# Fetching an expert's two rows with one gather of 8 KB per token, in a two-block transformer kernel

## The chip, the cores and the metric

The kernel runs as one program on one core of a Trainium2 chip. The metric is the time of one execution on the device, in microseconds (us). Three executions of the kernel before took 2143.99, 2161.14 and 2180.10 us; their median, 2161.14 us, is the time before. A profile of one execution shows what each engine did: TensorE (PE, matmuls), VectorE (DVE), ScalarE (ACT), GpSimd (POOL), SyncE (SP), and the 16 DMA engines that move data between HBM and SBUF.

## The reference, cut to what matters

A sequence of 256 tokens of width 1024 goes through a first block (modulated attention and pooling, then a convolutional feed-forward) and through a second model of two layers. Layer 0 has a hybrid attention (a sparse and a block-sparse one), layer 1 a latent attention with compressed keys. Each layer ends in a feed-forward of 16384 small experts, of which each token takes 16 in each of 8 heads. For a token `h` and its pick with table row `i` and weight `g` that is:

```
u = u_tab[i]                      # 1024 numbers, one row of 4 KB
v = v_tab[i]                      # 1024 numbers, one row of 4 KB
y += g * gelu(sum(u * h)) * v     # 8 heads x 16 picks for each token, in both layers
```

The rows are different for each token, so they are gathered by index. 2 layers x 256 tokens x 128 picks x 8 KB is 537 MB, three quarters of all that the kernel reads.

## The kernel before, in words

The program is written by hand engine by engine, with semaphores between engines. A function `order()` writes one list of steps, and each of the five engines walks the same list and does its own part of each step, in that order. An engine never takes a later step first: if its part of a step waits, all its later parts wait behind it.

**Tiles and picks.** Tokens form two tiles of 128, one token on each SBUF partition. A "round" is (layer, tile, head), and a pick is a round and a number j from 0 to 15, so there are 32 rounds and 512 picks. One gather (`L1699`, POOL) fetches for all 128 tokens the row of one table that their pick j names: 128 rows of 4 KB, 512 KB in all. There are 1024 gathers, 512 from each table. They land in a ring, `gring`, of NG = 16 slots of 4 KB on each partition. A gather waits until the slot's user 16 gathers earlier is done.

**A pick's work.** Step `u`: DVE multiplies the U row by the token and sums it (`dot`, L1537), which leaves one number on each partition in `acts`, and the slot is free. After 16 dots, step `gate`: ACT takes Gelu of the 16 numbers at once (L1054), DVE multiplies them by the 16 gate weights (L1544). Step `v`: for most picks ACT writes a 128x128 diagonal matrix of the 16 numbers' column (`diagonal`, L1063, one of four buffers, made two picks ahead), and PE multiplies it with the V row in two matmuls of 512 columns into an accumulating PSUM bank (L825 and L826). For the picks that `by_vector` names (odd j in the heads 0 to 3 except in the first two heads of all, and odd j in all heads of the last tile) DVE adds the scaled V row instead (L1556). The steps `v` of a round stand between the steps `u` of the next round, so V runs 16 picks behind U.

**What lies around.** The first block and the first tile's hybrid attention run before the first gather, until 556 us. After that the expert picks are dealt out between the steps of the rest (`together`, with `PACE`): while the experts of one tile run, the other tile's attention, its projections and its choice of experts (`pick`, on DVE, with one Exp on ACT, L1049) are computed. There are three such stages: layer 0 experts of tile 0 beside the hybrid attention of tile 1; layer 0 experts of tile 1 beside the latent attention of tile 0; layer 1 experts of tile 0 beside the latent attention of tile 1. At the end the experts of layer 1, tile 1 run with nothing beside them.

An attention is a series of 16 units, and the steps of unit u, the transposes of unit u-1 and the product with the values of unit u-2 stand together. A unit is: PE scores (L670), DVE adds the mask and takes the row maximum (L1338, L1345), ACT Exp (L1020), PE transposes (L566), ACT or DVE copy, PE product with the values (L687), DVE scaling (L1357). A projection (`mm`, L621) reads weights in loads of 1 MB, each with 4 x 128 rows of 512 numbers (2 KB), that SP issues into NW = 6 slots of `wring`. During the first block other parts of `gring` hold modulation vectors, gains and the last weights of the first feed-forward (`HELD`); their places are fixed column ranges.

## Time and profile before

| quantity | value |
|---|---|
| time of three executions, us | 2143.99, 2161.14, 2180.10 |
| median, us | 2161.14 |
| profiled execution: span from its first to its last instruction, us | 2111.6 |
| PE, DVE, ACT, POOL busy, us | 1648.0, 1375.4, 388.8, 1128.4 |
| gathers: packets, MB, share of the 16 DMA engines' time | 147456, 536.94, 65.0% |
| other loads: packets, MB, share | 106942, 182.85, 24.2% |
| first gather waits until, us | 556 |

The page has no other time of the profiled execution than its span, which is 49.5 us below the median of the three timed ones. The profile cuts the span in 40 slices of 52.8 us and says for each how busy an engine was. A gather has 128 data packets of 4 KB, eight on each DMA engine, and 16 small ones that raise the semaphore.

### The profile page before, as it was taken

The page shows a single profiled execution, that of the slowest core. Times are in us where ns is not written, and L with a number is a line of the kernel's source. Part 1 is how long each engine was busy: PE and PEld are TensorE (multiplying, and loading weights), DVE is VectorE, ACT ScalarE, POOL GpSimd, SP SyncE. Part 2 cuts the span into 40 slices and gives each one's busy share as a digit, 9 for nine tenths or more (in the row PEclk, how much of TensorE's full clock was granted, in tenths as well). Part 3 has the DMA queues.
Part 4 walks back from the last instruction along what each step waited for, and adds up shares of the span by engine and source line. Part 5 has one row for each costly group of instructions (what it writes and reads, how often), then busy time and mean ns, then how long its engine had stood idle before and what let it go on. Part 6 is the DMA issues. An engine that isn't in the chain of part 4 may idle for free.

```text
span 2111.6 us, 15758 instructions
## 1 busy us (share of the span) xinstructions
PE 1648.0 (78%) x4610; PEld 828.8 (39%) x4610; DVE 1375.4 (65%) x3269; ACT 388.8 (18%) x902; POOL 1128.4 (53%) x1028
## 2 busy tenths in 40 slices
PE   3997999998567978987876888878768996555565
PEld 1465887444233434432343433333434442111111
DVE  6564432142796695687757668776784887777775
ACT  1022000012121222222122222221322221100001
POOL 0000000000377577577766767776687777777773
PEclk9977999998789979999796999999788999887667
DMA  9851569162799999999999999999999999999997
GB/s 357 303 197 60 165 194 329 57 238 80 245 372 385 401 399 407 401 406 380 400 396 406 404 403 406 408 397 401 397 354 384 407 394 365 408 409 409 409 410 313
DMA packets 254483, 720.79 MB, mean 341 GB/s; under 512 B 24518, under 2 KB 49598, under 8 KB 253886
## 3 DMA queue, kind: packets, MB, share of 16 engines
q0 software_dynamic: 147456, 536.94, 65.0%
q1 hardware_dynamic: 106942, 182.85, 24.2%
q8 instruction: 38, 0.62, 0.1%
q14 instruction: 47, 0.39, 0.0%
HBM read 718.66 MB, written 1.05 MB: 341 GB/s over the span
## 4 chain that ended last, share of the span: by engine, by line
PE 40%; DMA 21%; POOL 17%; DVE 13%; issue 7%; ACT 2%; SPq 0%; POOLq 0%; DVEq 0%; ACTq 0%
POOL gring L1699 17%; DMA gring<-in_peer_v_dram,sel_idx 17%; PE PS L621 13%; PE PS L753 7%; PE PS L825 5%; PE PS L826 5%; DVE gring L1537 4%; PE PS L727 4%; PE PS L566 3%; DMA gring<-in_peer_u_dram,sel_idx 2%; DMA wring<-in_hyb_w_in_dram 1%; DVE xs L1556 1%; PE PS L670 1%; PE PS L687 1%; PE PS L706 1%
## 5 line engine op out<-in xcount | busy, mean ns | idle before, releaser
L1699 POOL DMA_INDIRECT gring<-in_peer_u_dram,sel_idx x512 | 566.0, 1105 | 725.1 <-DVE sel_g L1523 556.2
L825 PE MATMUL PS<-gring,diags 128*128 128x512 f32 x736 | 449.0, 695 | 321.3 <-DMA gring<-in_peer_v_dram,sel_idx 211.5
L1699 POOL DMA_INDIRECT gring<-in_peer_v_dram,sel_idx x512 | 562.2, 1098 | 230.3 <-issue 130.5
L1537 DVE CUSTOM_DVE_ANT_0 gring<-gring,hs 128x1024 f32<-128x1024 f32 x400 | 482.1, 1221 | 134.3 <-DMA gring<-in_peer_u_dram,sel_idx 133.1
L826 PE MATMUL PS<-gring,diags 128*128 128x512 f32 x736 | 434.2, 676 | 0.0
L621 PE MATMUL PS<-wring,hTs 128*128 128x512 f32 (+3 forms) x968 | 410.4, 574 | 9.8 <-DVE hTs L1125 4.3
L825 PEld LDWEIGHTS PS<-gring,diags 128*128 128x128 f32 x736 | 135.4, 210 | 545.4 <-issue 383.4
L621 PEld LDWEIGHTS PS<-wring,hTs 128*128 128x128 f32 x968 | 179.8, 195 | 219.8 <-issue 217.4
L826 PEld LDWEIGHTS PS<-gring,diags 128*128 128x128 f32 x736 | 158.8, 216 | 210.5 <-issue 210.5
L1063 ACT ACTIVATE diags<-consts,acts 128x128 f32<-128x128 f32 x368 | 136.4, 397 | 511.3 <-PE PS L826 476.8
L1537 DVE CUSTOM_DVE_ANT_0 gring<-gring,PS 128x1024 f32<-128x1024 f32 x112 | 136.4, 1220 | 70.4 <-DMA gring<-in_peer_u_dram,sel_idx 70.4
L753 PE MATMUL PS<-hTs,wring 128*128 128x256 f32 (+1 forms) x768 | 154.8, 365 | 1.9 <-DVE hTs L1101 1.9
L753 PEld LDWEIGHTS PS<-hTs,wring 128*128 128x128 f32 x768 | 137.5, 193 | 19.8 <-issue 2.3
L1556 DVE SCALAR_TENSOR_TENSOR xs<-gring,acts,xs 128x1024 f32<-128x1024 f32 x80 | 102.6, 1282 | 8.3 <-DMA gring<-in_peer_v_dram,sel_idx 8.1
L566 PE MATMUL PS<-consts,work 128*128 128x128 f32 (+1 forms) x344 | 67.2, 321 | 50.0 <-ACT work L1020 18.6
L950 ACT ACTIVATE work<-PS 128x512 f32<-128x512 f32 (+4 forms) x122 | 55.7, 463 | 222.0 <-PE PS L621 114.0
L1556 DVE SCALAR_TENSOR_TENSOR PS<-gring,acts,PS 128x1024 f32<-128x1024 f32 x62 | 79.9, 1288 | 12.3 <-DMA gring<-in_peer_v_dram,sel_idx 8.8
L566 PEld LDWEIGHTS PS<-consts,work 128*128 128x128 f32 (+1 forms) x344 | 48.5, 161 | 84.5 <-ACT work L1020 23.6
L1020 ACT ACTIVATE work<-work,small 128x128 f32<-128x128 f32 (+3 forms) x72 | 35.3, 490 | 226.2 <-DVE small L1345 226.2
L1148 DVE SCALAR_TENSOR_TENSOR gring<-wring,small,gring 128x512 f32<-128x512 f32 x84 | 63.1, 751 | 3.9 <-DMA wring<-in_w_ada_dram 1.1
L727 PE MATMUL PS<-gring,keep 128*128 128x512 f32 x120 | 55.0, 600 | 0.9 <-issue 0.9
L1338 DVE CUSTOM_DVE_ANT_0 work<-PS,consts 128x128 f32<-128x128 f32 (+1 forms) x72 | 25.5, 354 | 38.1 <-PE PS L670 37.4
(194 smaller groups left out, 1188.9 us busy)
## 6 DMA issues: line engine op xcount, KB each, us to landing
wring<-in_peer_w_q_dram SPq DMA_DIRECT2D x32, 1024.0 KB, 14.7
wring<-in_w_ada_dram SPq DMA_DIRECT2D x24, 1024.0 KB, 9.7
wring<-in_w_up_dram SPq DMA_DIRECT2D x44, 512.0 KB, 5.1
wring<-in_hyb_w_in_dram SPq DMA_DIRECT2D x20, 1024.0 KB, 8.3
wring<-in_w_in_dram SPq DMA_DIRECT2D x10, 1024.0 KB, 8.1
wring<-in_hyb_w_out_dram SPq DMA_DIRECT2D x8, 1024.0 KB, 19.2
gring<-in_peer_u_dram,sel_idx POOLq DMA_INDIRECT x512, 12.9
gring<-in_peer_v_dram,sel_idx POOLq DMA_INDIRECT x512, 13.4
```

The lines of the kernel that those rows point to most:

```text
L566: ins = pe.e.transpose(ps[0:c, 128 * i:128 * i + 128], s, ident)
L621: ins = pe.e.matmul(ps, lhs(k), slot[s][:, k - k0, 0:n], start=(k == 0), stop=(k == kt - 1))
L727: ins = pe.e.matmul(ps, gT[:, k, 128 * t:128 * t + 128], slot[s][:, k % 4, :], start=(k == first), stop=(k == last))
L753: ins = pe.e.matmul(PS[:, 512 * b + 256 * j + c0:512 * b + 256 * j + c0 + n], slot[s][:, k % 4, off + 128 * j:off + 128 * j + 128], hT[:, ...
L825: pe.e.matmul(ybank[0], d, row[i % NG][:, 0:512], start=first, stop=last)
L826: pe.e.matmul(ybank[1], d, row[i % NG][:, 512:1024], start=first, stop=last).then_inc(summed, 1)
L950: return ac.e.activation(dst, src, ACT.Copy)
L1063: ac.e.activation(d, ident, ACT.Copy, scale=acts[:, c:c + 1]).then_inc(diag_ready, 1)
L1148: ins = e.scalar_tensor_tensor(ac, slot[s][:, k % 4, :], cact[:, k:k + 1], ac, ALU.mult, ALU.add)
L1537: e.tensor_tensor_reduce(row[i % NG], row[i % NG], hbank if (l, t) == (1, 1) and hd else h[t], 1.0, 0.0, ALU.mult, ALU.add, acts[:, c:c + ...
L1556: e.scalar_tensor_tensor(x[t] if in_x or (hd, j) == (7, 15) else vbank, row[i % NG], acts[:, c:c + 1], x[t] if in_x or (hd, j) == (0, 1) e ...
L1699: gp.e.indirect_dma_start(out=row[i % NG], out_offset=None, in_=table, in_offset=bass.IndirectOffsetOnAxis(ap=sel_idx[:, c:c + 1], axis=0) ...
```

## The change

The two tables are laid side by side before the launch, so that U and V of an expert are one row of 8 KB (`peer_uv`). One gather per pick fetches both; there are 512 gathers of 1 MB. The ring has NG = 11 slots of 8 KB (88 KB on each partition, 64 before), and a slot is free when V of the pick has been used. V runs LAG = 2 picks behind U. The Gelu and the gate multiplication are done for each pick alone, both on ACT (new L1051 and L1054), and the diagonal of a pick (new L1066) is written by ACT in the step in which PE uses it. The weight ring has 4 slots instead of 6. To make room, the three late gain vectors share one buffer `late` that is loaded three times, and the first block's modulation vectors and gains lie in other columns of `gring`.

```diff
-NG = 16
-NW = 6
+NG = 11
+NW = 4
+ROW = 2 * D
+LAG = 2
...
+    picks = [(*r, j) for r in ROUNDS for j in range(16)]
     experts = []
-    waiting = []
-    for now, past in zip(ROUNDS + [None], [None] + ROUNDS):
-        if now == (1, 1, 1):
-            waiting = waiting + [("hold",)]
-        for j in range(16):
-            if now:
-                experts.append(waiting + [("u", *now, j)])
-                waiting = []
-            if past:
-                experts.append(waiting + [("v", *past, j)])
-                waiting = []
-        if now:
-            waiting = [("gate", *now)]
+    for n in range(len(picks) + LAG):
+        step = []
+        if n < len(picks):
+            if picks[n] == (1, 1, 1, 0):
+                step.append(("hold",))
+            step.append(("u", *picks[n]))
+        if n >= LAG:
+            step.append(("v", *picks[n - LAG]))
+        experts.append(step)
...
-    together(16 + 32 * 7, PACE[0], c00, hybrid(1), choose(1, 0))
-    together(16 + 32 * 8, 16.0, left.pop())
-    together(16 + 32 * 15, PACE[1], mla(0), choose(0, 1))
-    together(16 + 32 * 16, 16.0, left.pop())
-    together(16 + 32 * 23, PACE[2], mla(1), choose(1, 1))
-    together(16 + 32 * 24, 16.0, left.pop())
+    together(16 * 8 - 4, PACE[0], c00, hybrid(1), choose(1, 0))
+    together(16 * 9, 16.0, left.pop())
+    together(16 * 16 - 4, PACE[1], mla(0), choose(0, 1))
+    together(16 * 17, 16.0, left.pop())
+    together(16 * 24 - 4, PACE[2], mla(1), choose(1, 1))
+    together(16 * 25, 16.0, left.pop())
...
-        row = [gring[:, D * i:D * (i + 1)] for i in range(NG)]
-
-        gain = late + [gring[:, 13 * D:14 * D]]
+        urow = [gring[:, ROW * i:ROW * i + D] for i in range(NG)]
+        vrow = [gring[:, ROW * i + D:ROW * (i + 1)] for i in range(NG)]
+
+        gain = [gring[:, D * i:D * (i + 1)] for i in (9, 10, 11, 13)]
...
-        mod = gring[:, 0:6 * D]
+        mod = gring[:, 16 * D:22 * D]
...
-                i = gather_n[("v", l, t, hd, j)]
+                i = dot_n[(l, t, hd, j)] - 1
...
+                pe.e.matmul(ybank[0], d, vrow[i % NG][:, 0:512], start=first, stop=last)
+                pe.e.matmul(ybank[1], d, vrow[i % NG][:, 512:1024], start=first, stop=last).then_inc(summed, 1)
...
-            def gate(l, t, hd):
-                c0 = 128 * t + 16 * hd
-                ac.wait_ge(dotted, 16 * round_n[(l, t, hd)])
-                ac.e.activation(acts[:, c0:c0 + 16], acts[:, c0:c0 + 16], ACT.Gelu).then_inc(act_done, 1)
+            def gate(l, t, hd, j):
+                c = 128 * t + 16 * hd + j
+                n = dot_n[(l, t, hd, j)]
+                ac.wait_ge(dotted, n)
+                ac.e.activation(acts[:, c:c + 1], acts[:, c:c + 1], ACT.Gelu).then_inc(act_done, 1)
+                ac.wait_ge(chosen, chosen_n[(t, l, hd // 2)])
+                ac.wait_ge(act_done, n)
+                ac.e.activation(acts[:, c:c + 1], acts[:, c:c + 1], ACT.Copy,
+                                scale=sel_g[:, c:c + 1]).then_inc(weighted, 1)
 
             def diagonal(l, t, hd, j):
+                if by_vector(l, t, hd, j):
+                    return
                 c = 128 * t + 16 * hd + j
                 n = sum_n[(l, t, hd, j)]
                 d = diags[:, 128 * (n % 4):128 * (n % 4) + 128]
-                ac.wait_ge(weighted, round_n[(l, t, hd)])
+                ac.wait_ge(weighted, dot_n[(l, t, hd, j)])
                 if n > 4:
                     ac.wait_ge(summed, n - 4)
                 ac.e.activation(d, ident, ACT.Copy, scale=acts[:, c:c + 1]).then_inc(diag_ready, 1)
...
-            def expert(l, t, hd, j):
-
-                mine = [i for i in range(16) if not by_vector(l, t, hd, i)]
-                if j == 0:
-                    for i in mine[:2]:
-                        diagonal(l, t, hd, i)
-                if j in mine:
-                    for i in mine[mine.index(j) + 2:mine.index(j) + 3]:
-                        diagonal(l, t, hd, i)
...
+                u = urow[i % NG]
+                e.tensor_tensor_reduce(u, u, hbank if (l, t) == (1, 1) and hd else h[t], 1.0, 0.0, ALU.mult, ALU.add,
                                        acts[:, c:c + 1]).then_inc(dotted, 1)
-
-            def gate(l, t, hd):
-                c0 = 128 * t + 16 * hd
-                ve.wait_ge(act_done, round_n[(l, t, hd)])
-                ve.wait_ge(chosen, chosen_n[(t, l, hd // 2)])
-                e.tensor_tensor(acts[:, c0:c0 + 16], acts[:, c0:c0 + 16], sel_g[:, c0:c0 + 16],
-                                ALU.mult).then_inc(weighted, 1)
 
             def expert(l, t, hd, j):
                 if by_vector(l, t, hd, j):
-                    n, i = add_n[(l, t, hd, j)], gather_n[("v", l, t, hd, j)]
+                    n, i = add_n[(l, t, hd, j)], dot_n[(l, t, hd, j)] - 1
                     c = 128 * t + 16 * hd + j
-                    ve.wait_ge(weighted, round_n[(l, t, hd)])
-                    ve.wait_ge(row_landed[i % NG], 16 * (i // NG + 1))
...
+                if name == "h0":
+                    group(l_late, (late[:, :], a["ffn_norm_2"][0].partition_broadcast(128)))
+                if name == "m0":
+                    sp.wait_ge(h_ready, h_n["c10"])
+                    group(l_late, (late[:, :], a["ffn_norm_2"][1].partition_broadcast(128)))
+                if name == "fin0":
+                    sp.wait_ge(h_ready, h_n["c11"])
+                    group(l_late, (late[:, :], a["final_norm_2"].partition_broadcast(128)))
...
-            def gather(kind, table, l, t, hd, j):
-                i = gather_n[(kind, l, t, hd, j)]
+            def gather(l, t, hd, j):
+                i = dot_n[(l, t, hd, j)] - 1
                 c = 128 * t + 16 * hd + j
                 if i >= NG:
-                    before = gathers[i - NG]
-                    if before[0] == "u":
-                        gp.wait_ge(dotted, dot_n[before[1:]])
-                    elif by_vector(*before[1:]):
-                        gp.wait_ge(row_added, add_n[before[1:]])
+                    before = picks[i - NG]
+                    if by_vector(*before):
+                        gp.wait_ge(row_added, add_n[before])
                     else:
-                        gp.wait_ge(summed, sum_n[before[1:]])
+                        gp.wait_ge(summed, sum_n[before])
                 else:
                     gp.wait_ge(late_down, 1)
-                if i == 5:
+                if i == NG - 1:
                     gp.wait_ge(x_ready, x_n["g1"])
                 gp.wait_ge(chosen, chosen_n[(t, l, hd // 2)])
-                gp.e.indirect_dma_start(out=row[i % NG], out_offset=None, in_=table,
+                gp.e.indirect_dma_start(out=gring[:, ROW * (i % NG):ROW * (i % NG + 1)], out_offset=None, in_=table,
                                         in_offset=bass.IndirectOffsetOnAxis(ap=sel_idx[:, c:c + 1], axis=0)
...
+    given["peer_uv"] = np.concatenate([inputs["peer_u_2"], inputs["peer_v_2"]], -1)
```

The first place is ACT's own order in the attention of tile 1 in layer 0, beside head 3 of the experts: three units before. L1020 is the Exp of a unit, L950 the copy of the transposes, L1063 a diagonal; words in brackets are the semaphores that a row waits for.

```order
L1020 ACTIVATE work,small<-work,small 128x256 [waits top_ready]
L950 ACTIVATE work<-PS 128x256 [waits full0]
L1063 ACTIVATE diags<-consts,acts 128x128 [waits summed]
L1020 ACTIVATE work,small<-work,small 128x256 [waits top_ready]
L950 ACTIVATE work<-PS 128x256 [waits full2]
L1020 ACTIVATE work,small<-work,small 128x256 [waits top_ready]
L950 ACTIVATE work<-PS 128x256 [waits full5]
```

The same engine and place after the change, two units. L1016 is the Exp, L946 the copy, L1051 the Gelu, L1054 the gate weight, L1066 the diagonal.

```order
L1016 ACT_TABLE_LOAD
L1016 ACTIVATE work,small<-work,small 128x256 [waits top_ready]
L946 ACTIVATE work<-PS 128x256 [waits full2]
L1051 ACT_TABLE_LOAD
L1051 ACTIVATE acts<-acts 128x1 [waits dotted]
L1054 ACTIVATE acts<-acts,sel_g 128x1 [waits act_done]
L1051 ACTIVATE acts<-acts 128x1 [waits dotted]
L1054 ACTIVATE acts<-acts,sel_g 128x1 [waits act_done]
L1066 ACTIVATE diags<-consts,acts 128x128 [waits summed,weighted]
L1016 ACT_TABLE_LOAD
L1016 ACTIVATE work,small<-work,small 128x256 [waits top_ready]
```

Between two Exps there is now a Gelu for each pick, which waits for that pick's dot (`dotted`), and a table load on either side of the Gelus; the diagonal stands behind them. In the whole program ACT has 157 table loads, 67 before.

The second place is PE's order in the same attention, after the change. L667 are the scores of the next unit, L563 the transposes, L684 the product with the values, L822 and L823 the V matmuls.

```order
L822 MATMUL PS<-gring,diags 128x512 [waits row_landed3,diag_ready]
L823 MATMUL PS<-gring,diags 128x512
L667 MATMUL PS<-keep,hTs 128x256 [waits emptied1]
L563 MATMUL PS<-consts,work 128x128 [waits exp_done]
L563 MATMUL PS<-consts,work 128x128
L684 MATMUL PS<-keep,work 128x64 [waits emptied3,emptied5]
L684 MATMUL PS<-keep,work 128x64
L667 MATMUL PS<-keep,hTs 128x256 [waits emptied4]
```

As before, the scores of the next unit stand behind the V matmuls, and these wait for `diag_ready`; what has moved is the diagonal, which was written two picks ahead and now follows the Gelu of the pick two later.

The third place is ACT beside the choice of experts of tile 1 (layer 0), before: L950 copies a projection's result, L1049 is the Exp of the gate weights.

```order
L950 ACTIVATE work<-PS 128x512 [waits full2]
L950 ACTIVATE work<-PS 128x512 [waits full3]
L1063 ACTIVATE diags<-consts,acts 128x128 [waits summed] x8
L1049 ACT_TABLE_LOAD
L1049 ACTIVATE sel_g<-sel_g 128x32 [waits gate_in]
L1063 ACTIVATE diags<-consts,acts 128x128 [waits summed] x2
L950 ACTIVATE work<-PS 128x512 [waits full5]
L950 ACTIVATE work<-PS 128x512 [waits full0]
```

And after the change, from the same Exp on:

```order
L1045 ACT_TABLE_LOAD
L1045 ACTIVATE sel_g<-sel_g 128x32 [waits gate_in]
L1051 ACT_TABLE_LOAD
L1051 ACTIVATE acts<-acts 128x1 [waits dotted]
L1054 ACTIVATE acts<-acts,sel_g 128x1 [waits act_done]
L1066 ACTIVATE diags<-consts,acts 128x128 [waits summed,weighted]
L946 ACTIVATE work<-PS 128x512 [waits full5]
L946 ACTIVATE work<-PS 128x512 [waits full0]
L1051 ACTIVATE acts<-acts 128x1 [waits dotted]
```

The copies of a projection wait for PE (`full`), and the Gelu and the diagonal that PE's next V matmul needs stand behind them.

## Rows read from the trace of the kernel before

**Rows 1.** The page: slices and DMA queues (packets, MB, share of the engines).

```profile
GB/s 357 303 197 60 165 194 329 57 238 80 245 372 385 401 399 407 401 406 380 400 396 406 404 403 406 408 397 401 397 354 384 407 394 365 408 409 409 409 410 313
DMA packets 254483, 720.79 MB, mean 341 GB/s; under 512 B 24518, under 2 KB 49598, under 8 KB 253886
...
q0 software_dynamic: 147456, 536.94, 65.0%
q1 hardware_dynamic: 106942, 182.85, 24.2%
```

**Rows 2.** Busy time by stretch: stretch, its length, engines, clock, DMA share, GB/s.

```profile
325.00:340.00 15.00, 15.00 (x71) 13.22 (x70) 4.37 (x9) 0.63 (x1) 0.00 (x0) 1.00 1.04 388
...
1850.00:2050.00 200.00, 116.65 (x156) 37.06 (x156) 145.08 (x201) 14.80 (x44) 150.85 (x161) 0.72 1.03 409
...
88.00:90.00 2.00, 2.00 (x6) 0.92 (x5) 0.00 (x0) 0.00 (x0) 0.00 (x0) 1.00 1.08 452
```

**Rows 3.** Gathers of 1850 to 2050 us: idle before them, time to landing.

```profile
  issue: 45.7, 150
...
DMA to landing us min/median/max: 9.5/12.9/16.4
```

**Rows 4.** Busy time in two stretches in which the DMA rate is lower.

```profile
590.00:640.00 50.00, 40.22 (x104) 18.51 (x104) 46.21 (x154) 9.66 (x24) 39.63 (x35) 0.89 1.01 388
1540.00:1590.00 50.00, 34.72 (x104) 19.32 (x103) 39.85 (x83) 12.17 (x31) 40.16 (x33) 0.80 0.95 340
```

**Rows 5.** Gathers of 590 to 640 us: idle before them by releaser.

```profile
  issue: 10.4, 34
```

**Rows 6.** Busy time in the three attention stretches.

```profile
732.00:812.00 80.00, 57.14 (x173) 27.29 (x172) 69.01 (x177) 23.61 (x64) 59.95 (x52) 0.81 1.03 402
1094.00:1165.00 71.00, 47.99 (x121) 26.18 (x120) 51.74 (x137) 19.21 (x63) 50.76 (x45) 0.69 1.03 401
1483.00:1572.00 89.00, 60.06 (x176) 33.67 (x174) 70.83 (x161) 23.42 (x67) 66.98 (x53) 0.79 1.00 376
```

**Rows 7.** Time line of one attention unit, from its mask to its dots.

```profile
767.43 0.42 DVE L1338 CUSTOM_DVE_ANT_0 work<-PS,consts 128x256 f32<-128x256 f32 x1
...
768.08 0.51 ACT L1020 ACTIVATE work<-work,small 128x256 f32<-128x256 f32 x1 [4.21 <-DVE small L1345]
768.15 0.28 DVE L1357 TENSOR_SCALAR work<-PS,small 128x64 f32<-128x64 f32 x1
768.35 1.22 DVE L1537 CUSTOM_DVE_ANT_0 gring<-gring,hs 128x1024 f32<-128x1024 f32 x1
...
768.59 0.36 ACT L950 ACTIVATE work<-PS 128x256 f32<-128x256 f32 x1
...
769.49 1.28 DVE L1556 SCALAR_TENSOR_TENSOR xs<-gring,acts,xs 128x1024 f32<-128x1024 f32 x1
```

**Rows 8.** Groups of the whole span: busy us and mean ns, idle before.

```profile
L825 PE MATMUL PS<-gring,diags 128*128 128x512 f32 x736 | 449.0, 695 | 321.3 <-DMA gring<-in_peer_v_dram,sel_idx 211.5 <-ACT diags L1063 109.4
...
L1063 ACT ACTIVATE diags<-consts,acts 128x128 f32<-128x128 f32 x368 | 136.4, 397 | 511.3 <-PE PS L826 476.8 <-DVE acts L1544 34.3
...
L670 PE MATMUL PS<-keep,hTs 64*128 64x128 f32 (+3 forms) x128 | 40.0, 397 | 0.9 <-DVE keep L1101 0.9
...
L1054 ACT ACT_TABLE_LOAD x25 | 32.1, 1283 | 0.4
...
L1054 ACT ACTIVATE acts<-acts 128x16 f32<-128x16 f32 x32 | 6.9, 216 | 204.9 <-DVE acts L1537 204.8
```

**Rows 9.** Time line of PE beside a projection.

```profile
860.19 1.02 PE L825 MATMUL PS<-gring,diags 128*128 128x512 f32 x2
...
861.91 3.60 PE L621 MATMUL PS<-wring,hTs 128*128 128x512 f32 x8
```

**Rows 10.** DMA queues from 700 to 730 us.

```profile
q0 software_dynamic: 2134, 7.78, 65.6%
q1 hardware_dynamic: 2132, 4.24, 37.5%
```

49 lines of the change are left out of this document (16 added, 33 removed).

## The prediction

> **What bounds the kernel now.** I read the page's 40 slices first. From the 12th slice on the DMA engines move 354 to 410 GB/s and are busy in all ten tenths [rows 1]; the gathers alone are 536.94 MB and 65.0% of the engines' time. So from 556 us on the kernel is a stream of gathers, and everything else is dealt out beside it. Then I looked at a stretch with nothing else in it: from 1850 to 2050 us the rate is 409 GB/s [rows 2], and POOL idles 45.7 us for its own issue and almost nothing for slots, while a gather takes 12.9 us to land [rows 3]. At 409 GB/s a gather of 524288 B takes 1.282 us, so some ten are in flight: the queue is deep and the DMA engines are the bound, but POOL is close behind (150.85 us busy and 45.7 us of issue in 200). Third, the slices with a lower rate: 388 GB/s at 590 us and 340 at 1540 us [rows 4]. At 590 us POOL is busy 39.63 us and idle 10.4 us for issue, which is the whole 50 us [rows 5]; there POOL bounds, with the DVE at 46 of 50 us next to it. Fourth, the three attention stretches, 80 + 71 + 89 = 240 us long [rows 6]: in two of them the DMA engines still run at 401 to 402 GB/s, but DVE is busy 69 of 80 us in the first. The 81 picks that the step list deals out there thus take 240 us; the other 431 are bound by bytes.
>
> **Bytes of the gathers.** A packet of 2 KB (weights alone, 388 GB/s) takes 16 x 2048 / 388 = 84.5 ns of its engine, one of 4 KB (gathers alone, 409 GB/s) 160.2 ns [rows 2]. The second 2 KB cost 75.7 ns, so the line through both gives 160.2 + 2 x 75.7 = 311.6 ns for 8 KB: a pick takes 8 x 311.6 = 2.49 us on each engine instead of 2 x 1.282 = 2.56. That is 0.07 us for each of 431 picks, **-31 us**. The ends are 0 (nothing gained by length) and the stretch at 88 us, where loads with 8 KB rows run beside others at 452 GB/s [rows 2]: 2.32 us a pick, -105 us. I take the line, since it rests on long stretches.
>
> What shows that a row of 8 KB can be one packet: 254483 - 253886 = 597 packets are not under 8 KB [rows 1], and three loads of `b_ada` and one of the pooling band, 128 such rows each, are 512 of them; they were issued by SP, though, not by POOL. The Trainium skill ("DMA: Bandwidth & Descriptors", section "SWDGE vs HWDGE vs iDMA") says that a packet made by GpSimd is preferably at most 4096 B; by that a row would be cut in two, this term would be 0 and the sum 31 us higher. The packet count of the changed kernel's first queue decides it.
>
> **POOL.** It issues 512 gathers instead of 1024. An issue and its gap took (150.85 + 45.7) / 161 = 1.22 us for 512 KB at the least [rows 2, 3], and will serve 1 MB; POOL stops being a bound. The slices under 400 GB/s after the 12th miss about 200 GB/s x 52.8 us / 405 = 26 us [rows 1]; DVE is nearly full in one of them and one is attention, so I take 10 of these 26: **-10 us**.
>
> **Attention.** Here the change adds a wait. ACT takes a pick's Gelu behind its dot, and the diagonal of the pick two before stands behind that Gelu; PE's V matmul waits for the diagonal, and PE's scores of the next unit, which DVE needs to go on, stand behind the V matmul. So DVE and PE take turns where they ran side by side. One lap, from the end of the scores: mask and maximum to the Exp 0.65 us (767.43 to 768.08), Exp 0.51, copy 0.36 [rows 7]; table load 1.28, Gelu 0.22, gate weight taken like it 0.22, diagonal 0.40 [rows 8]; that is 3.65. The dot of the first pick is over at 2.1 (769.49 against 767.43) and hides. V takes 1.72 us back to back at full clock (860.19 to 861.91, rows from [rows 9]); all V matmuls together take 2 x 449 / 368 = 2.44 us each, the second half taken like the first [rows 8]. The clock in the attention stretches is 0.81, 0.69 and 0.79 [rows 6], so I take 2.2. Scores are 0.40, handovers 0.25. The lap:
> - one V on PE before the next scores: 3.65 + 2.2 + 0.65 = 6.5 us; the step list has 23 such units of the 45;
> - two V on PE: 8.8 us, 8 units;
> - DVE's add and a second dot ahead of the one V on PE: the second dot ends at 2.06 + 1.28 + 1.22 = 4.56, then Gelu, weight, diagonal 0.84, V 2.2, scores and handovers 0.65: 8.2 us, 9 units;
> - only a DVE pick: 2.06 + 1.28 + 0.55 = 3.9 us, 5 units.
>
> Sum 23 x 6.5 + 8 x 8.8 + 9 x 8.2 + 5 x 3.9 = 313 us, less 5 for the smaller tile 0, is 308 against 240: **+68 us**. Bytes do not bound there any more (81 x 2.49 = 202 us, and little weight). With V at 1.72 the same sum is 284, +44; the lower end is 0, if the turns overlap more than the order says. Table loads rise from 67 to 157, 90 x 1.28 = 115 us of ACT, most of it inside these laps; ACT is busy 388.8 us of 2111.6 and has no bound of its own outside them.
>
> **Projections beside the later heads.** PE is gapless at 858 to 865 us: V, V, then 3.60 us for a 1 MB load of weights [rows 9]. Now, when a projection's last matmul is done, ACT copies it (0.5), and only then come a Gelu, a weight and the diagonal for PE's next V (0.84), with handovers 1.6 us of PE standing. There are 6 such results in each of three stages beside heads that leave all V to PE, 18 x 1.6 = 29 us; DMA time hides some (PE is not always gapless), I take **+22 us**, ends 0 and 50 (where DVE makes the copy and the dot of 1.22 us follows it, the gap is 3 us).
>
> **The rest.** In the first block 4 weight slots hold 2 MB less ahead, 5.4 us at 388 GB/s [rows 2], once or not at all where the loads are short: +4, ends 0 and 11. The end: after the last landing now come dot, Gelu, weight, add: 1.22 + 0.22 + 0.22 + 1.28 instead of 1.28, +2. Together **+6**. DVE loses 32 gate multiplications, nothing on the path. The gains loaded by SP late in the list wait for norms long done, 0.
>
> **Sum.** -31 - 10 + 68 + 22 + 6 = +55 us on the profiled execution: 2111.6 to 2167 us. The three timed executions lie 32 to 69 us above that span; I add the same difference to their median: 2161 + 55 = **2216 us**, 2.5% slower. Own range of this case 2172 to 2260 (V at 1.72 and a gap of 0 give 2170).
>
> **Rivals.**
> - *The stream stays the bound (faster).* If the eight or so rows that are in flight or landed ahead bridge the laps, and DMA runs on at full rate, the change gives 512 x 0.07 = -36, POOL -26, and +6: 2161 - 56 = 2105 us. For it: in the attention stretches DMA was at 401 GB/s although DVE was 86% busy. Against it: a ring bridges one slow lap (8 x 2.49 = 20 us), not 15 in a row. It decides if a unit with two picks closes in 5 to 5.5 us. A chance of 0.22.
> - *Long packets are worth more.* With 452 GB/s: -105 in place of -31, 2142 us. 0.08.
> - *Weights starve.* From 700 to 730 us both queues have work, and they get 2134 and 2132 packets: one for one, 4 KB against 2 KB, so weights got 4.24 MB in 30 us, 141 GB/s [rows 10]. One for one with 8 KB leaves them a fifth, some 84 GB/s, 12.5 us for 1 MB instead of 7.4, and there are 4 slots to look ahead instead of 6. My sum has nothing for it, since PE that waits for weights stops freeing ring slots, the gathers run dry after 20 us and the weights get everything; bytes are moved all the time. If that gap costs PE 7 us at each of 6 starts of a run of projections, +42: 2258 us. 0.13. The Trainium skill (same page, section "Queues, rings and completion order") says that a DMA engine switches between queues by packets; the packet counts agree.
> - *The row is cut into 4 KB packets*, the page's rule above: the gather term is 0, and the time 2161 + 86 = 2247 us. 0.10.
>
> **Chances.** The forecast has 0.47. What is within 2% of 2161 (2118 to 2204) is about what a measurement here can't tell from no change. Faster: most of the first rival, 0.20. Within: two fifths of the forecast, the second rival, a little of the first and the others, 0.33. Slower: 0.47. The range from 2105 to 2262 us leaves about a tenth on either side.
>
> **What would show it.** First queue: 65536 + 8192 packets if rows stay whole, and a pure stretch at the end at 421 GB/s. POOL busy near 560 us. Attention laps of 6.5 to 8.8 us between Exps, DMA well under 400 GB/s there, DVE idle there for PE's scores, and PE's V matmuls waiting for ACT's diagonals by far more than 109 us. The forecast is wrong if the three attention series still take about 240 us, or if PE waits for weight loads.

## The result and the profile after

Four executions of the changed kernel took 2331.22 to 2336.83 us, median **2333.34 us**; the kernel before, on the same chip, 2156.47. The ratio is 1.081, with a 95% interval from 1.0767 to 1.0852: the change makes the kernel 8% slower. The forecast had the direction and less than a third of the size (+55 us; +177 measured), and its range ended at 2262.

The page of the changed kernel, whose profiled execution has a span of 2335.0 us (2111.6 before): slices, then queues.

```profile
PEclk9978899998899667999797689998867999887777
...
GB/s 293 318 144 74 162 144 261 167 100 162 401 348 399 268 210 221 322 408 368 361 406 303 228 284 384 416 419 410 394 243 274 308 379 361 419 422 421 422 421 302
...
q0 software_dynamic: 73728, 536.90, 58.0%
q1 hardware_dynamic: 106942, 182.85, 22.1%
```

73728 is 65536 + 8192: the 8 KB rows travel whole. The last slices show 421 and 422 GB/s, where 409 stood before [rows 1]. What is new is in the middle: three holes of 210 to 308 GB/s, at the three attention stretches, in which the clock granted to PE is low too.

Groups of instructions of the whole span after (busy us, mean ns, idle before and its releaser), the answer to [rows 8]:

```profile
L1679 POOL DMA_INDIRECT gring<-in_peer_uv_dram,sel_idx x512 | 564.8, 1103 | 1739.0 <-PE PS L823 1014.5
L822 PE MATMUL PS<-gring,diags 128*128 128x512 f32 x736 | 488.7, 751 | 444.5 <-ACT diags L1066 426.0
```

Waits after, in total, times and longest:

```profile
POOL gring L1679 <- PE PS L823: 1014.5, 335, 17.1
...
PE PS L822 <- ACT diags L1066: 426.0, 170, 8.9
...
DVE work L1331 <- PE PS L667: 206.9, 60, 7.4
```

PE waits 426 us for diagonals, four times the 109.4 of [rows 8]; DVE waits 206.9 us for scores; POOL waits for slots, not for its own issue.

**Where the 223 us of the profile went.** I cut each execution at the first and last Exp of the three attention series beside the experts (hybrid tile 1; latent tile 0; latent tile 1), read from ACT's time line. Lengths in us; the columns "between" are mostly projections and the choice of experts:

| kernel | up to hybrid | hybrid | between | latent 0 | between | latent 1 | to the end | span |
|---|---|---|---|---|---|---|---|---|
| before | 735.9 | 76.3 | 281.7 | 70.3 | 319.3 | 87.2 | 540.9 | 2111.6 |
| changed | 781.6 | 141.9 | 326.2 | 103.3 | 340.5 | 121.3 | 520.2 | 2335.0 |
| before, 4 weight slots | 784.2 | 78.1 | 284.2 | 66.5 | 333.5 | 90.9 | 565.6 | 2203.0 |
| diagonal first | 778.9 | 107.7 | 301.9 | 78.1 | 332.7 | 76.8 | 502.0 | 2178.1 |
| diagonal first, 6 weight slots | 742.5 | 108.6 | 301.9 | 76.0 | 328.1 | 76.3 | 506.5 | 2139.9 |
| two diagonals first, lag 3, 6 slots | 741.0 | 100.4 | 295.4 | 73.9 | 326.2 | 85.7 | 508.7 | 2131.3 |
| Gelu in fours, lag 6, 4 slots | 769.1 | 90.2 | 302.3 | 66.9 | 333.2 | 74.5 | 515.7 | 2151.9 |
| changed, PE kept busy | 778.3 | 120.8 | 316.2 | 89.4 | 338.3 | 93.8 | 516.7 | 2253.5 |
| two diagonals first, PE kept busy | 745.2 | 94.3 | 295.9 | 67.2 | 324.3 | 80.2 | 515.0 | 2122.1 |
| changed, again | 784.3 | 140.2 | 327.1 | 101.7 | 342.3 | 122.5 | 515.7 | 2333.8 |

Changed minus before: +45.7 until the hybrid, +132.7 in the three attention stretches, +65.7 between them, -20.7 at the end. That is 223 us, and the medians are only 177 apart: the profiled execution of the kernel before is a short one (2111.6, beside a median of 2156.47), that of the changed kernel is not (2335.0, beside 2333.34). With the last group of runs below the kernel before took 2110.79 us and the changed one 2336.03, which is 225 apart. The third row is the old form with the weight ring of the changed one. Against it the changed kernel is 2.6 us shorter until the hybrid, 131.0 longer in the three attention stretches, 49.0 longer between them and 45.4 shorter at the end; the end of the third row is long by dips in its DMA rate, which the section on two gathers shows.

The same stretches of the changed kernel (length, PE, PEld, DVE, ACT, POOL, clock, DMA share, GB/s), with [rows 6] as their counterpart:

```profile
781.60:923.50 141.90, 87.35 (x196) 38.70 (x196) 64.77 (x167) 70.08 (x150) 31.68 (x29) 0.68 0.58 204
923.50:1249.70 326.20, 257.59 (x627) 115.96 (x626) 208.37 (x522) 107.33 (x321) 105.00 (x91) 0.88 0.94 371
1249.70:1353.00 103.30, 53.37 (x115) 28.49 (x115) 49.72 (x131) 61.44 (x127) 25.95 (x23) 0.66 0.65 229
...
1693.50:1814.80 121.30, 77.56 (x180) 41.83 (x180) 65.32 (x150) 69.16 (x149) 30.92 (x31) 0.70 0.69 253
```

DVE, 64.77 of 141.90 us busy, and DMA, at 204 GB/s, have both stopped being near a bound. The clock is 0.68, 0.66 and 0.70. One lap shows it, on the time line of the hybrid stretch (start, length, engine, line):

```profile
884.60 0.42 DVE L1331 CUSTOM_DVE_ANT_0 work<-PS,work 128x256 f32<-128x256 f32 x1 [6.48 <-PE PS L667]
...
885.25 0.51 ACT L1016 ACTIVATE work<-work,small 128x256 f32<-128x256 f32 x1 [4.75 <-DVE small L1338]
...
886.14 1.28 ACT L1051 ACT_TABLE_LOAD   x1
...
887.87 0.39 ACT L1066 ACTIVATE diags<-consts,acts 128x128 f32<-128x128 f32 x1
...
888.31 2.07 PE L822 MATMUL PS<-gring,diags 128*128 128x512 f32 x2 [2.99 <-ACT diags L1066]
...
890.18 1.91 PE L823 MATMUL PS<-gring,diags 128*128 128x512 f32 x2
...
891.88 1.86 PE L822 MATMUL PS<-gring,diags 128*128 128x512 f32 x2
...
893.58 1.02 PE L823 MATMUL PS<-gring,diags 128*128 128x512 f32 x2
...
894.54 0.48 PE L667 MATMUL PS<-keep,hTs 64*128 64x256 f32 x1
```

From the mask to PE's V it is 888.31 - 884.60 = 3.71 us, as forecast (3.65). But PE had stood idle 2.99 us, and its clock was low: the first V pair takes 888.31 to 891.88 = 3.57 us, about twice the 1.72 of [rows 9]. Two picks take 6.2 us until the next scores, where I had put 4.4. This is one of the slow laps: on PE's time line V's four matmuls take 3.23 us on average over the 47 picks whose V is on PE in the three stretches.

### The profile page after: what moved, and what is told of

It reads as the page before. It is cut to its first block, busy times and chain, and to the rows that moved or that the text cites. A ratio compares the mean times of both kernels' runs of the same rounds, so it can differ in the third digit from the quotient of the medians.

```text
span 2335.0 us, 16628 instructions
## 1 busy us (share of the span) xinstructions
PE 1740.6 (75%) x4610; PEld 862.6 (37%) x4610; DVE 1361.1 (58%) x3237; ACT 720.1 (31%) x1984; POOL 565.0 (24%) x516
## 3 DMA queue, kind: packets, MB, share of 16 engines
q0 software_dynamic: 73728, 536.90, 58.0%
## 4 chain that ended last, share of the span: by engine, by line
PE 48%; DVE 21%; DMA 16%; ACT 8%; issue 5%; POOL 1%; SPq 0%; DVEq 0%; ACTq 0%; POOLq 0%
PE PS L618 12%; DMA gring<-in_peer_uv_dram,sel_idx 10%; PE PS L822 10%; PE PS L823 9%; DVE gring L1531 7%; PE PS L750 7%; PE PS L724 3%; PE PS L563 3%; ACT L1051 2%; PE PS L667 2%; ACT diags L1066 2%; DVE xs L1542 1%; DMA wring<-in_hyb_w_in_dram 1%; DMA wring<-in_mla_w_ukv_dram 1%; POOL gring L1679 1%
## 5 line engine op out<-in xcount | busy, mean ns | idle before, releaser
L1679 POOL DMA_INDIRECT gring<-in_peer_uv_dram,sel_idx x512 | 564.8, 1103 | 1739.0 <-PE PS L823 1014.5
L822 PE MATMUL PS<-gring,diags 128*128 128x512 f32 x736 | 488.7, 751 | 444.5 <-ACT diags L1066 426.0
L1531 DVE CUSTOM_DVE_ANT_0 gring<-gring,hs 128x1024 f32<-128x1024 f32 x400 | 475.7, 1218 | 21.7 <-DMA gring<-in_peer_uv_dram,sel_idx 20.7
L823 PE MATMUL PS<-gring,diags 128*128 128x512 f32 x736 | 465.9, 721 | 0.0
L618 PE MATMUL PS<-wring,hTs 128*128 128x512 f32 (+3 forms) x968 | 416.7, 580 | 27.2 <-DMA wring<-in_hyb_w_in_dram 6.6
L822 PEld LDWEIGHTS PS<-gring,diags 128*128 128x128 f32 x736 | 143.8, 221 | 687.6 <-ACT diags L1066 587.1
L1051 ACT ACTIVATE acts<-acts 128x1 f32<-128x1 f32 x512 | 102.9, 201 | 745.4 <-DVE acts L1531 738.4
L823 PEld LDWEIGHTS PS<-gring,diags 128*128 128x128 f32 x736 | 170.2, 231 | 231.8 <-issue 231.8
L750 PE MATMUL PS<-hTs,wring 128*128 128x256 f32 (+1 forms) x768 | 163.3, 377 | 16.3 <-DMA wring<-in_w_up_dram 14.4
L1054 ACT ACTIVATE acts<-acts,sel_g 128x1 f32<-128x1 f32 x512 | 150.8, 295 | 17.6
L1066 ACT ACTIVATE diags<-consts,acts 128x128 f32<-128x128 f32 x368 | 142.1, 386 | 1.4 <-PE PS L823 1.1
L946 ACT ACTIVATE work<-PS 128x512 f32<-128x512 f32 (+4 forms) x122 | 55.4, 463 | 166.2 <-PE PS L618 66.8
L1016 ACT ACTIVATE work<-work,small 128x128 f32<-128x128 f32 (+3 forms) x72 | 35.3, 490 | 205.2 <-DVE small L1338 195.9
L563 PE MATMUL PS<-consts,work 128*128 128x128 f32 (+1 forms) x344 | 70.3, 332 | 31.4 <-ACT work L946 11.1
L1094 DVE COPY work<-PS 128x256 f32<-128x256 f32 (+3 forms) x34 | 16.0, 470 | 103.7 <-PE PS L618 56.0
## 6 DMA issues: line engine op xcount, KB each, us to landing
wring<-in_hyb_w_out_dram SPq DMA_DIRECT2D x8, 1024.0 KB, 13.8
```

The lines of the kernel that those rows point to most:

```text
L563: ins = pe.e.transpose(ps[0:c, 128 * i:128 * i + 128], s, ident)
L618: ins = pe.e.matmul(ps, lhs(k), slot[s][:, k - k0, 0:n], start=(k == 0), stop=(k == kt - 1))
L750: ins = pe.e.matmul(PS[:, 512 * b + 256 * j + c0:512 * b + 256 * j + c0 + n], slot[s][:, k % 4, off + 128 * j:off + 128 * j + 128], hT[:, ...
L822: pe.e.matmul(ybank[0], d, vrow[i % NG][:, 0:512], start=first, stop=last)
L823: pe.e.matmul(ybank[1], d, vrow[i % NG][:, 512:1024], start=first, stop=last).then_inc(summed, 1)
L1051: ac.e.activation(acts[:, c:c + 1], acts[:, c:c + 1], ACT.Gelu).then_inc(act_done, 1)
```

## The experiments

The runs were measured in three groups, each with the kernel before beside it on the same chip, and each ratio is to the kernel before of its own group. That kernel took 2151.4 us in the first group (the next four sections), 2114.76 in the second (the two after them) and 2110.79 in the third; the changed kernel took 2333.34 us beside 2156.47, and 2336.03 in the third group. So across groups I compare kernels of the new form by their times and stretches rather than by ratios, and differences of some ten us across groups are not safe.

### The diagonal ahead of the Gelu

```diff
-            for s in steps:
+            mine = list(steps)
+            for n in range(len(mine) - 1):
+                if mine[n][0] == "u" and mine[n + 1][0] == "v":
+                    mine[n], mine[n + 1] = mine[n + 1], mine[n]
+            for s in mine:
```

> The changed kernel with one difference: in ACT's list the diagonal of pick n-2 stands ahead of the Gelu of pick n, not behind it. Theory 'order' (the lap dot, Gelu, diagonal, V matmul, scores costs the time): where two V matmuls stand between two units, the first diagonal no longer waits for the table load and the new dot; the lap of about 10 us in the attention of layer 0 should fall to about 7, the series of 16 Exps from 142 us to 100 to 115, the other two by 10 to 20 us each, and the gaps of PE behind a projection shrink; the time falls from 2333 to 2230 to 2280 us. Rival 'tables' (the 90 more table loads cost it): the number of loads is the same 157, so the time stays within 15 us of 2333.

Measured: 2170.77 us, ratio 1.0093 (1.0073 to 1.0114). This swap on ACT alone takes back 163 us, more than the 53 to 103 expected; the two latent stretches fell by 25 and 44 us where 10 to 20 each were expected. The same kind of lap in the hybrid stretch:

```profile
852.93 0.39 ACT L1066 ACTIVATE diags<-consts,acts 128x128 f32<-128x128 f32 x1
853.34 1.28 ACT L1051 ACT_TABLE_LOAD   x1
...
853.38 1.12 PE L822 MATMUL PS<-gring,diags 128*128 128x512 f32 x2 [1.25 <-ACT diags L1066]
...
855.51 1.13 PE L822 MATMUL PS<-gring,diags 128*128 128x512 f32 x2
...
857.43 0.70 PE L667 MATMUL PS<-keep,hTs 64*128 64x256 f32 x2
```

The diagonal is out before the table load, PE idles 1.25 us instead of 2.99, and in this lap its V runs at full clock. The lap from scores to scores is 857.43 - 850.67 = 6.8 us (10.7 before the swap, from 883.86 to 894.54). In the stretches as a whole the clock rises less in the first two than in the third:

```profile
778.90:886.60 107.70, 78.17 (x196) 35.01 (x196) 64.51 (x167) 70.04 (x149) 33.12 (x29) 0.75 0.76 272
1188.50:1266.60 78.10, 46.75 (x115) 25.14 (x115) 49.20 (x131) 61.35 (x126) 25.24 (x22) 0.69 0.82 299
1599.30:1676.10 76.80, 53.78 (x180) 30.76 (x180) 64.84 (x150) 68.58 (x149) 36.52 (x31) 0.91 0.96 390
```

The three stretches are 103.9 us shorter together. V's 47 picks take 120.1 us in them instead of 151.6, so some 31 of the 103.9 us are V at a higher clock, and the rest is the shorter wait ahead of it.

### Gelu left out

```diff
-                ac.e.activation(acts[:, c:c + 1], acts[:, c:c + 1], ACT.Gelu).then_inc(act_done, 1)
+                ac.e.activation(acts[:, c:c + 1], acts[:, c:c + 1], ACT.Copy).then_inc(act_done, 1)
```

> The changed kernel with Copy in place of the expert's Gelu (the Gelu is left out, so this is a time without that function's table). ACT then has hardly any table load beside the experts. 'Tables': the lap loses 1.28 us ahead of the Gelu and another ahead of the next Exp, up to 2 x 1.28 x 45 units = 115 us, and more elsewhere: 2333 falls to 2200 or below. 'Order': only the load between the copy and the Gelu is on the lap, 45 x 1.28 = 58 us at the most, the waits for dots and the V matmuls stay: 2270 to 2300 us.

Measured: 2298.32 us, ratio 1.0689 (1.0663 to 1.0715). The table loads between Gelu and Exp cost 35 us of the 177, 7 us of it in the hybrid stretch (134.7 against 141.9) and 22 in the three attention stretches (344.8 against 366.5). They lengthen the laps, and are not the main thing. One reason stands on the time line: in a lap without the load the Gelu comes 2.29 us after the mask (877.39 - 875.10) and has waited 0.77 us for the dot; with it, 2.83 us (887.43 - 884.60). The dot hides more than half of the load.

### The kernel before with four weight slots

```diff
-NW = 6
+NW = 4
```

> The kernel before with 4 weight slots instead of 6 and nothing else. If the slots alone made the first gather 26 us later (582 against 556 us) and cost nothing later, the time is 2156 + 20 to 30 = 2176 to 2186 us, with the first gather at 575 to 585 us. If weight loads starve beside the gathers ('weights starve'), PE's waits for wring rise by tens of us behind 583 us and the time is above 2200.

Measured: 2202.86 us, ratio 1.024 (1.021 to 1.0269), +51 us, above both the 2176 to 2186 expected and the 2200 from which the rival begins. Up to the hybrid it takes 784.2 us, as the changed kernel does. Waits of PE and DVE for weights in this kernel until 560 us; in the kernel before no wait for `w_up` is listed there, and those for `w_ada` are 4.3 us in all:

```profile
PE PS L753 <- DMA wring<-in_w_up_dram: 15.2, 4, 4.0
DVE gring L1148 <- DMA wring<-in_w_ada_dram: 13.6, 3, 8.0
DVE gring L1146 <- DMA wring<-in_w_ada_dram: 4.7, 2, 3.5
```

Behind 583 us PE waits 13.8 us for weights in this kernel, 0.5 in the kernel before and 15.3 in the changed one. So weights do come late beside the gathers, but not by the tens of us of the rival; +48.3 of the +51 us stand ahead of the hybrid.

### Two gathers of 4 KB into the same slots

```diff
-                gp.e.indirect_dma_start(out=gring[:, ROW * (i % NG):ROW * (i % NG + 1)], out_offset=None, in_=table,
...
+                for dst, table in ((urow[i % NG], utab), (vrow[i % NG], vtab)):
+                    gp.e.indirect_dma_start(out=dst, out_offset=None, in_=table,
```

> The changed kernel with its rows fetched by two gathers of 4 KB rows into the two halves of the same slot; everything else as changed. This prices the 8 KB row alone. If long rows give only the rate (421 against 409 GB/s where bytes bound), about 250 picks of 512 are bound by bytes in the changed kernel: +15 to +20 us, 2350 us. If POOL's issue of 1.24 us and more for each gather binds too, up to +40, 2373 us. Where laps bound, no difference.

Measured: 2397.15 us, ratio 1.114 (1.1115 to 1.1165): one gather per pick is worth 64 us within this kernel, more than the 31 + 10 of my sum and outside what was expected (2350 to 2373). The pure stretch in this kernel and, in the second fence, in the changed one:

```profile
2100.00:2300.00 200.00, 103.63 (x142) 33.67 (x143) 130.83 (x179) 45.98 (x179) 134.56 (x144) 0.76 0.97 377
```

```profile
2080.00:2280.00 200.00, 113.88 (x161) 35.49 (x162) 146.41 (x200) 51.58 (x200) 76.05 (x81) 0.77 1.01 422
```

In 200 us 72 picks against 81; POOL is busy 134.56 us for the 72. The 377 GB/s lie below the 409 of [rows 2] though the gathers have the same size. The same 200 us in 40 slices show why: most slices are at 404 to 415 GB/s, and three dips go down to 145, 209 and 153.

```profile
GB/s 408 410 410 410 410 410 404 145 313 388 412 410 409 412 407 407 413 408 347 209 288 330 415 409 414 409 407 410 411 410 383 320 153 320 400 415 412 409 406 414
```

By the rates alone, 422 against 409, it would be 78 picks against 81; the dips cost the other six of the nine, so about two thirds of what the one gather gains in this stretch are dips that it does not have. The kernel before with four weight slots has such dips too, and its end is long for it:

```profile
1850.00:2050.00 200.00, 106.97 (x158) 34.99 (x156) 144.09 (x211) 18.12 (x46) 136.57 (x144) 0.80 0.99 381
```

Both forms issue 1024 gathers, and only in the profiles of these two does an engine wait for something that the profile calls remote. POOL in the latter:

```profile
POOL gring L1699 <- remote: 28.1, 8, 5.1
```

ACT's diagonals wait 79.3 us for it there. The profile of the kernel before, also with 1024 gathers, has no such wait, and its stretch from 1850 to 2050 us stays at 405 GB/s and above in every slice; none of the eleven profiles with 512 gathers has one either. What makes the dips is not known.

### V six picks behind U

```diff
-LAG = 2
+LAG = 6
```

> The changed kernel with V six picks behind U instead of two (LAG = 6) and ACT's list otherwise as changed: the diagonal of pick n-6 stands behind the Gelu of pick n. Theory 'order': what PE waits for is not the age of its own pick but the Gelu of the newest pick that stands ahead of the diagonal on ACT, so a longer lag gives little: 2300 to 2350 us, and PE's wait for diagonals stays above 350 us. Rival 'lag' (two picks are too few to hide dot, Gelu and diagonal): the time falls to 2170 to 2230 us.

Measured: 2414.8 us, ratio 1.1438 (1.1409 to 1.1468), some 80 us slower than the changed kernel and above the 2300 to 2350 expected. PE's wait for diagonals is 464.0 us, above 350 as expected. The attention stretches stay at 139.0, 103.1 and 120.4 us: distance alone does nothing, because the old diagonal still stands behind the newest Gelu. What grows is the rest: 698.3 us between them (666.7 in the changed kernel) and 564.8 at the end (520.2). A slot is now held until six further picks have had their dot and Gelu, and the ring has eleven. DVE's waits for gathers in this kernel, then in the changed one:

```profile
DVE gring L1531 <- DMA gring<-in_peer_uv_dram,sel_idx: 251.2, 161, 5.5
```

```profile
DVE gring L1531 <- DMA gring<-in_peer_uv_dram,sel_idx: 85.8, 67, 2.7
```

The longer wait alone does not prove the harm, as the run with Gelu in fours below has nearly as much of it. The rate does: the last full slices of this run are at 383 to 399 GB/s, those of the changed kernel at 421 to 422.

### Mended order without Gelu, with six weight slots, and with Gelu in fours

Without Gelu the edit is the two above together. For six weight slots:

```diff
-NG = 11
-NW = 4
+NG = 9
+NW = 6
```

Gelu in fours: ACT takes four picks at once a step after the fourth dot, DVE multiplies by the four gate weights a step later, diagonals stand ahead of the Gelu, and V runs six picks behind.

```diff
+LAG = 6
+GB = 4
...
+                ac.wait_ge(dotted, GB * (k + 1))
+                ac.e.activation(acts[:, c:c + GB], acts[:, c:c + GB], ACT.Gelu).then_inc(act_done, 1)
```

> The diagonal ahead of the new Gelu (as in e1_diag_first), and Copy in place of the expert's Gelu (Gelu left out). What the table loads cost once the order is mended: in the laps of 6.7 us the load still stands ahead of the second diagonal where one of the two is a DVE pick. Without loads: 2171 falls by 15 to 35 us, to 2136 to 2156. If it falls by under 8 us, the loads are hidden and the order was all.

> As e1_diag_first, but with 6 weight slots as before and a ring of 9 slots of 8 KB (the first block's vectors moved so that they fit in 72 KB). If 4 weight slots cost what they cost in the kernel before (51 us, of which 33 ahead of the first gather), the first gather comes back to 556 us and the time falls to 2130 to 2145 us. If a ring of 9 is too short to bridge the laps, that is lost again in part and the time is 2145 to 2175.

> The changed kernel with Gelus in groups of four picks (one ACT instruction of 128x4, one DVE multiplication by the gate weights), V six picks behind U, the diagonal ahead of the group's Gelu on ACT; 104 table loads. Theory 'order': as e1_diag_first and with fewer loads, 2140 to 2165 us. Against it: with V six picks behind, only 4 or 5 of 11 slots can be in flight, and if that leaves the DMA engines dry in the laps the time is above 2180.

Measured: 2157.44 us (ratio 1.0203, 1.018 to 1.0226), 2142.37 us (1.015, 1.0124 to 1.0176) and 2159.0 us (1.0241, 1.0196 to 1.0287).

- Without Gelu it is 13 us less than with the diagonal first alone, between the two answers that were expected (15 to 35, or under 8), and measured in another group. The three attention stretches take 248.9 us instead of 262.6. So with the mended order the table loads cost little, but not nothing.
- Six slots bring the hybrid's start back to 742.5 us (778.9 with four), as expected, and the ring of nine costs nothing that the stretches show.
- Groups of four shorten the hybrid stretch to 90.2 us. The three attention stretches take 231.6 us together, no more than the 233.8 of the kernel before. What this run still loses, 769.1 us against 735.9 until the hybrid, it loses mostly in the part where the four weight slots alone cost 48.3; groups of four with six slots were not run. A lag of six does no harm there, as its diagonals do not stand behind the newest dot: the last full slices of that run are at 415 to 422 GB/s, although DVE waits for gathers nearly as long as with the lag of six alone:

```profile
DVE gring L1535 <- DMA gring<-in_peer_uv_dram,sel_idx: 232.1, 165, 8.1
```

### Both older diagonals ahead of both Gelus

With LAG = 3, NG = 9 and NW = 6; the core of the edit:

```diff
+                if m == n + 4 and [s[0] for s in mine[n:m]] == ["u", "v", "u", "v"]:
+                    mine[n:m] = [mine[n + 1], mine[n + 3], mine[n], mine[n + 2]]
```

> The changed kernel with V three picks behind U, six weight slots and nine row slots, and on ScalarE, where two picks follow each other, both older diagonals ahead of both newer Gelus. If the coupling on ScalarE is what is left of the loss in the attention stretches (in the run with the single diagonal first and six slots the Exps of the hybrid attention's second tile still stood 108.6 us apart from first to last, in the kernel before 76.3), they come to 80 to 90 us and the whole to 2105 to 2125 us, about the kernel before. If it is something else there (the table loads, the two tasks of DVE), the stretch stays at 100 to 109 us and the whole at 2140 to 2150 us, and six row slots ahead instead of seven cost a few us more.

Measured: 2132.4 us, ratio 1.0082 (1.0049 to 1.0114). The hybrid stretch came to 100.4 us, not to 80 to 90: most of what the mended order still loses in it is not this coupling, and what it is stays open. The three attention stretches take 260.0 us together, as with the single diagonal first and six slots (260.9), because the last one is 9.4 us longer; and as the lag changed too, the 10 us that this run is shorter are not the pairs' alone.

### TensorE kept busy, and the changed kernel again

```diff
+                if after_attention[0] and (l, t, hd, j) not in first_sum:
+                    for _ in range(FILL):
+                        pe.e.matmul(ybank[0], blank, wide, start=False, stop=False)
+                after_attention[0] = False
                 pe.wait_ge(diag_ready, n)
```

> The changed kernel as it is, but before the first V after a step of attention TensorE multiplies three times by a block of zeros (128x512, added to the sum, so that nothing changes in it) instead of idling. Theory: half of what the attention laps lost beside my forecast is that V ran at half clock because TensorE stood idle for 3 us ahead of it; then the granted clock in the attention stretches rises from 0.66 to 0.70 to over 0.85, V's pair of matmuls there falls from 1.9 to 1.1 us, the stretch of the hybrid's second tile from 141.9 to 110 to 120 us, and the whole gains 40 to 70 us against the changed kernel on this chip. Rival: the lap's length is set by the order of waits on ScalarE and VectorE and the clock is only its consequence; then the clock rises but the stretch keeps 135 to 150 us, and the whole stays within 15 us or is slower by the three matmuls.

> The changed kernel again, on the chip of this call, so that the run with the multiplications by zeros can be compared with it directly. Every theory: 2320 to 2345 us, the Exps of the hybrid attention's second tile 139 to 143 us apart, clock 0.86.

Measured: 2266.9 us (ratio 1.0733, 1.0677 to 1.079), and the changed kernel 2336.03 us (1.1054, 1.0996 to 1.1112): **69 us less, by doing more** (40 to 70 expected; the rival had at most 15). The attention stretches of the run with the multiplications:

```profile
778.30:899.10 120.80, 103.35 (x275) 45.75 (x276) 64.72 (x167) 70.05 (x150) 31.65 (x29) 0.90 0.67 239
1215.30:1304.70 89.40, 66.52 (x182) 31.70 (x183) 49.71 (x131) 61.43 (x127) 25.31 (x23) 0.90 0.72 265
1643.00:1736.80 93.80, 84.07 (x266) 41.80 (x266) 65.26 (x150) 68.79 (x149) 35.29 (x31) 1.00 0.87 327
```

The clock is 0.90, 0.90 and 1.00 and they are 60 us shorter together (304.0 against 364.4 of the changed kernel in the same group). A lap on PE in it; L824 is the added work, L830 and L831 are V:

```profile
866.75 2.79 PE L824 MATMUL PS<-consts 128*128 128x512 f32 x6
869.90 1.13 PE L830 MATMUL PS<-gring,diags 128*128 128x512 f32 x2 [0.35 <-ACT diags L1076]
870.86 1.02 PE L831 MATMUL PS<-gring,diags 128*128 128x512 f32 x2
871.72 1.02 PE L830 MATMUL PS<-gring,diags 128*128 128x512 f32 x2
872.58 1.02 PE L831 MATMUL PS<-gring,diags 128*128 128x512 f32 x2
873.53 0.70 PE L668 MATMUL PS<-keep,hTs 64*128 64x256 f32 x2
```

Two picks of V now take 873.53 - 869.90 = 3.6 us instead of 6.2, and the lap 8.1 us. The order of the waits is unchanged, so this part is the clock's alone. Two granted levels show here: 1.02 us for a pair of matmuls at 2.4 GHz, 1.86 to 2.07 where the clock had fallen.

Over the three stretches V accounts for nearly all of it. PE's busy time in V's first and second lines, in the changed kernel, then in the run with the multiplications:

```profile
sum 366.50, PE 86.99 PEld 22.37; mean PE 29.00 PEld 7.46
sum 366.50, PE 81.47 PEld 28.97; mean PE 27.16 PEld 9.66
sum 304.00, PE 56.70 PEld 15.74; mean PE 18.90 PEld 5.25
sum 304.00, PE 53.26 PEld 19.45; mean PE 17.75 PEld 6.48
```

That is 168.5 against 110.0 us for the same 47 picks, 58.5 less.

### Pairs and busy TensorE together

The two edits above in one kernel.

> Both edits together: pairs of diagonals ahead of the Gelus, V three picks behind, six weight slots, and the three multiplications by zeros. If the clock still costs something with the mended order (0.75 in the hybrid's second tile there with the single diagonal first), 5 to 20 us faster than the same kernel without them; if TensorE hardly waits any more, the three multiplications are in the way and it is 5 to 20 us slower.

Measured: 2125.23 us, ratio 1.0067 (1.0043 to 1.0092). That is 7 us less than without the multiplications, but the two intervals overlap (2122.99 to 2136.61 us without, 2121.35 to 2133.21 with them), so the gain is not shown in the whole time. In its profile the clock of the three attention stretches is 0.98 to 1.00, and they take 241.7 us instead of 260.0. This is the lowest time of the forms with 8 KB rows, still 14 us above the kernel before in its own group; none beat it.

## Why the prediction was wrong, point by point

- **Direction and mechanism: right.** The wait for the diagonal behind the Gelu was the named mechanism; putting the diagonal ahead takes back 163 of 177 us (of 225, against the kernel before in its later groups). Of the signs that I had named, packets, 421 GB/s, POOL at 565 us, laps, low DMA rate and PE's wait are there. The rival with a cut row did not come about, nor the faster ones.
- **Attention, +68 forecast, +132.7 measured: the step that failed is "The clock in the attention stretches is 0.81, 0.69 and 0.79 [rows 6], so I take 2.2."** V took 3.23 us on average over the 47 picks on PE, 1.03 more than 2.2, which is 48 us: 308 + 48 = 356, and 366.5 was measured. Two things went wrong in that step. The 2.2 was low already for the kernel before: on its own time line V takes 2.69 us on average in the 39 picks that lie whole in these stretches, where I had lowered 2.44, a mean of the whole span, toward the 1.72 of a back-to-back stretch. That is 23 of the 48 us. The other 25 are the clock itself, carried over from the kernel before (0.81, 0.69, 0.79) to one whose PE idles for 3 us ahead of V in laps like the one shown, and where it fell to 0.68, 0.66 and 0.70. With PE kept busy V takes 2.04 us, the same sum gives 300, and 304.0 was measured. The lap's other part was right to 0.06 us (3.71 for 3.65). Of the +132.7, 6 us are only that the forecast counted the stretches before as 240 us and the table as 233.8.
- **Between the attentions, +22 forecast, +65.7 measured.** With the diagonal first, +33.6 are left; so the diagonal behind the Gelu cost 32 us there. That it is the wait at a projection's end, which I had put at 29 before its discount, is argued and not shown. Against the kernel before with four weight slots it is +49.0 instead of +65.7. For the rest, part of what the term left out is work that lies in another stretch. From the last Exp of the hybrid to the first of the latent attention the bytes are, in the kernel before, the changed one and the one with diagonal first and six slots:

```profile
DMA packets 36740, 112.19 MB, mean 398 GB/s; under 512 B 4186, under 2 KB 4186, under 8 KB 36726
```

```profile
DMA packets 26585, 120.95 MB, mean 371 GB/s; under 512 B 2959, under 2 KB 2959, under 8 KB 14847
```

```profile
DMA packets 26168, 120.10 MB, mean 398 GB/s; under 512 B 2944, under 2 KB 2944, under 8 KB 14434
```

  8.8 MB more at 398 GB/s are 22 of the 44.5 us in this stretch, the lower rate the other half. Of the 8.8 MB, 5.5 are gathers (96.04 MB against 90.50) and 3.2 are weights. The end moved the other way: 210.99 MB before, 200.82 after; 10.2 MB less at 390 GB/s are 26 us, more than its whole gain of 20.7. That the new limits of `together` and V close behind U deal the picks out earlier fits this, but no run tests it. Such a shift moves time between stretches and makes none.
- **Until the hybrid, +4 forecast, +45.7 measured: "once or not at all" failed, the second step that did.** The kernel before with four weight slots shows +48.3 there by itself, and six slots in the changed form (with the diagonal first) leave +6.6. I had priced 2 MB of lookahead as one load time, in the first block alone. About 26 us of it lie there (the first gather starts at 583 us instead of 557), with waits for several loads of `w_ada` and of `w_up`, which are 4.3 us and none before; the rest comes behind the first gather.
- **Gathers, -31 - 10: right in rate; the worth is not settled.** The line through the two packet lengths gave 421 GB/s, and 421 to 422 stand there. Against two gathers in the same form one gather is worth 64 us, a good part of it because the run with two has dips in its DMA rate that the kernel before does not have in its pure stretch. At the end of the program, where the term should show, the gain is 20.7 us against the kernel before and 45.4 against the one with four weight slots, and both ends hold more bytes than the changed kernel's.
- **From the span to the median: failed.** I added 49.5 us to the forecast because the timed executions of the kernel before lay above its span. For the changed kernel the median lies on its span, so the addition rested on a short profiled execution of the kernel before. With that term gone the forecast would have been 2167 us, further off still: the terms of the sum missed 223 - 55 = 168 us, and the addition hid 50 of them by luck.
- **Table loads: in the place assumed, at less than the price.** I had them inside the laps, at 1.28 us each; they are 35 us of the loss with the order as it was, since the dot hides part of them, and some 13 with the order mended.
- **Weights starving: small, right to leave it out.** PE's waits for weights behind 583 us rose from 0.5 to 15.3 us, where the rival had +42. By my own sign, "if PE waits for weight loads", the forecast would be wrong, but they are not what made it so.
- **The cut row: it did not come about.** The Trainium skill ("DMA: Bandwidth & Descriptors", section "SWDGE vs HWDGE vs iDMA") prefers packets by GpSimd of at most 4096 B; here 8192 B went whole and ran faster per byte, so the measurement decides against the cut for this kernel.

What stays open: why the hybrid stretch needs 94 to 108 us in every form with the mended order and a Gelu for each pick, against 76.3 before, and 90.2 with groups of four. Part of it is more work in the stretch: gathers are issued for 29 picks instead of some 26, and as V follows U closely, V's of other heads fall into it, 20 on PE and 9 on DVE where there were 15 and 12. Five more V on PE at 2.6 us, their mean there with the diagonal first, are 13 us; that is an estimate, which no run tests.

## What to carry to other kernels

When a change adds a wait ahead of TensorE, price the matmuls behind it from rows with such a wait (here 3.2 to 3.6 us for a V), not at the mean clock of the old trace. On an engine that works in order, write what others wait for (here the older diagonal) ahead of what must itself wait for the newest data; one swap was worth more than all that the change had aimed at. And when a buffer is made smaller to pay for another, try the old kernel with the small buffer alone: it showed 48 us ahead of the first attention stretch where the argument had put 4.
